# Reordered splits, squares, values and last tile pairs, and shifted convolution bounds, in a two-layer encoder kernel

## The chip, the cores and the metric

One NeuronCore of a Trainium2 chip runs the whole kernel. The metric is the device time of one execution in microseconds (us); the median of several executions is compared.

## What is computed

Two layers of an encoder over 256 positions and 1024 channels, all in fp32. Each layer, cut to what matters here:

```python
h = rmsnorm(x, attn_norm_g[l])
q, k, v, conv_in, gate_logits = jnp.split(h @ w_in[l], SPLITS, axis=-1)
q, k = apply_rope(q), apply_rope(k)            # rotate halves by cos/sin of the positions
y_attn = sliding_window_sink_attention(q, k, v, attn_sinks[l]) @ w_attn_o[l]
ca, cb = jnp.split(conv_in, 2, axis=-1)
u = causal_dwconv(ca * sigmoid(cb), conv_dw_w[l], conv_dw_b[l])      # 31 taps
y_conv = silu(layernorm(u, ...)) @ w_conv_o[l]
x = x + (sigmoid(g_attn) * y_attn + sigmoid(g_conv) * y_conv) @ w_out[l]
up = causal_dwconv(rmsnorm(x) @ w_ffn_up[l], ...)                     # 3 taps
x = x + (silu(gt) * val) @ w_ffn_down[l]
```

A final RMSNorm ends it.

## The kernel before

Weights come in units of 128 x 2048 numbers (16 blocks of 128 x 128), 66 units a layer, through a ring of three slots (`raw`, `whi`, `wlo`; unit u lies in slot u % 3). To keep fp32 accuracy each weight and each activation is split into a high part of type fp32r and the rest: the high part of a weight is `whi` (ScalarE, ACT in the profile, `split_high`, L311), the rest `wlo` (GpSimd, POOL, `split_low`, L250; in the last part of a layer VectorE, DVE, takes two of three, L891). A product of one block is three matmuls (L1034 to L1036): whi with high, whi with low, wlo with high. A unit is 48 matmuls of 256 columns. SyncE loads the next unit into a slot when `wlo` of the one before is written.

Every engine has its own queue of instructions, written out by hand and worked off in order; semaphores tie them. So the order of the lines is the schedule.

Units 0 to 7 give the convolution's input, 8 gives k and v, 9 to 12 give q, 13 to 20 the gates, 21 to 32 the three output projections, 33 to 65 the channel mixer ("FFN"). The steps that the change touches:

- **Start of layer 0.** DVE copies x and writes its low parts, then makes the angles of the rotation (L712 to L716; seven steps counted by the semaphore `table`; unit 2 on TensorE, PE, waits for them at L1191 since they use its bank `pu[2]`), then adds up the squares of x (`add_first_squares`, L692). PE multiplies units 0, 1 and 2 by parts (`unit_by_parts`, L1089) with x as it is; after unit 1 it sums the squares over partitions (`first_total`, L1184). ACT turns the sum into `rstd` (L356), and DVE then scales and normalises x for unit 3 (`normalise`, L655).
- **Rotations.** For k and for four pairs of q tiles, ACT writes the halves exchanged into `pt` (`swap_halves`, L445, four copies) and, behind that, splits the next unit for the slot just read (`next_high`, L317; for some units it also makes two products of a convolution that GpSimd adds up, L343, `tap_product`). DVE rotates (`rotate`, L767: two products and a sum). Between the rotations DVE works on the 31-tap convolution (`conv`, L723; a step is two taps, L749), in numbers of steps set by `CONV_BOUNDS`, one row a layer. In layer 0 ACT also makes sine and cosine after the first exchange.
- **Attention groups 0 to 7.** For each group PE multiplies a gate unit, transposes the probabilities (L1157), and multiplies them with the values of the group before (`values`, L1160). PE makes the scores of two groups at a time (L1146) inside every second gate unit, and waits there for the exponentials of the group before (L1137). DVE takes the maxima and the denominators with `conv` steps between them (7 steps a group in the first groups, 6 in the others, so that all 109 are done; L824).
- **End of a layer.** The last unit (65, slot 2) multiplies the last two hidden tiles (`ab` 0 and 1) into four banks (L1318 to L1327); it waits until both tiles are split. ACT loads the table for the roots, splits slots 0 and 1 for the next layer (L598), then squares x and writes its high parts as each bank is ready; DVE adds x and writes the low parts (L1002 to L1015). GpSimd makes `wlo` of slots 0, 1, 2 in that order.

Of the kernel before, what the change touches and what calls it, by code (L numbers as in the profile page):

```python
# [5 lines left out]
DEPTH, D_MODEL, SEQ = 2, 1024, 256  # L6
# [6 lines left out]
FT = D_FF // P  # L13
N_CHUNKS = SEQ // CHUNK
N_PAIRS = N_HEADS // 2
GROUPS = N_CHUNKS * N_KV
# [7 lines left out]
U_AO, U_CO, U_OUT, U_FFN = 21, 25, 29, 33  # L24
FFN_STEPS = FT // 2
UNITS = U_FFN + 3 * FFN_STEPS
AHEAD = 2
PIECES = 4
PIECE = UNIT // PIECES
UNSCALED = RING  # L30
# [3 lines left out]
USES = UNITS // RING  # L34
# [12 lines left out]
CONV_PAIRS, POOL_TILE, LAST_TILE = ((0, 1), (3, 4), (5, 6)), 2, 7  # L47
FIRST_TAPS = (TAPS + 1) // 2
CONV_STEPS = TAPS * len(CONV_PAIRS) + FIRST_TAPS
CONV_BOUNDS = ((37, 43, 49, 53, 56), (39, 45, 51, 55, 59))  # L50
CONV_DONE = (2 * TAPS, 4 * TAPS, 6 * TAPS, 2 * CONV_STEPS)
PRODUCT_BUFFERS = 3
PRODUCT_UNITS = (7, 8, 9, 10, 11, 12, 14, 16, 17, 18, 19, 20, 21, 22)
# [21 lines left out]
def hybrid_encoder(nc, x_in, pos_in, const_in, par_in, gf_in, w_in, y_out):  # L75
# [3 lines left out]
    with ctx:  # L79
# [98 lines left out]
        def finished(l, u):  # L178

            return uses(l, u) + 1  # L180
# [126 lines left out]
        def _(act):  # L307
# [3 lines left out]
            def split_high(l, s, n):  # L311

                act.wait_ge(raw_in[s], (l * USES + n) * 16)
                act.wait_ge(unit_done[s], l * USES + n)
                A(whi[s][:, :], raw[s][:, :], ACT.Copy).then_inc(hi_ready[s], 1)  # L315

            def next_high(l, u):  # L317
                if u + RING < UNITS:
                    split_high(l, (u + RING) % RING, (u + RING) // RING)
                if u + RING in PRODUCT_UNITS:  # L320
                    n = PRODUCT_UNITS.index(u + RING)
                    if n == 0:
                        tap_product(l, 0)
                    tap_product(l, n + 1)
                    if n == PRODUCTS - 3:
                        tap_product(l, n + 2)
# [84 lines left out]
            for l in range(DEPTH):  # L411
                par = par_all[:, l * NPAR:(l + 1) * NPAR]
                for i in range(NT):
                    u = U_GLU + i
# [30 lines left out]
                def swap_halves(n, src, tiles, scale):  # L445

                    if n:
                        act.wait_ge(rope_done, l * 10 + 2 * n)
                    for block in range(4):
                        rows, other = slice(32 * block, 32 * block + 32), slice(32 * (block ^ 1), 32 * (block ^ 1) + 32)  # L450
                        last = A(pt[rows, 0:tiles, :], src[other], ACT.Copy, scale=scale if block % 2 else -scale)
                    last.then_inc(rot_done, 1)

                u = U_KV
                act.wait_ge(unit_done[u % RING], finished(l, u))
                act.wait_ge(u_ready, l * NT + NT)
                swap_halves(0, pu[u % RING][:, 0:1, :], 1, HEAD_DIM ** -0.5)
                A(kvraw[:, 1, :], pu[u % RING][:, 1, :], ACT.Copy).then_inc(kv_raw, 1)
                next_high(l, u)
                if l == 0:  # L460
                    act.wait_ge(table, TABLE_STEPS)
                    A(sin[:, :], angles, ACT.Sin).then_inc(act_table, 1)
# [3 lines left out]
                for i in range(4):  # L466
                    u = U_Q + i
                    act.wait_ge(unit_done[u % RING], finished(l, u))
                    swap_halves(1 + i, pu[u % RING][:, :, :], 2, 1.0)
                    if i == 1:  # L470
                        act.wait_ge(vt_done, l + 1)
                        A(vwin[0:CHUNK, 0, :], po[0:CHUNK, 0, 0:P], ACT.Copy).then_inc(v_ready, 1)
                        A(vwin[:, 1:N_CHUNKS, :], po[:, :, :].rearrange("p a (b t) -> p (a b) t", t=P)[:, 1:N_CHUNKS, :], ACT.Copy).then_inc(v_ready, 1)
                    next_high(l, u)

                def evict_transposed(n):
                    act.wait_ge(tr_done, l * GROUPS + n + 1)
# [79 lines left out]
                def hidden_tile(k, ab, gcol, vcol, before=None, split=None):  # L557

                    act.wait_ge(up_ready, k + 1)
                    if before is not None:  # L560
                        act.wait_ge(f_ready, before)
                    for half, col in ((0, gcol), (1, vcol)):
                        A(fbuf[:, ab, half, :], up[:, ab, half, :], ACT.Identity, scale=par[:, col + 2:col + 2 + 1],  # L563
                          bias=par[:, col + 3:col + 3 + 1]).then_inc(f_conv0, 1)
                    if split is not None:
                        split()
                    act.wait_ge(f_tap, k * 4 + 3)
                    A(fbuf[:, ab, 2, :], fbuf[:, ab, 0, :], ACT.Silu).then_inc(f_silu, 1)
# [11 lines left out]
                def ffn_step(j, parity, last):  # L580

                    k = j * 2 + l * FT
                    col = j * 8 + PA_FW
                    hidden_tile(k, 0, col, col + FT * 4, k - 1, lambda: split_high(l, 2, j + 11))
                    act.wait_ge(unit_done[1], l * USES + j + 11)
                    hidden_high(k, 0, parity)
                    hidden_tile(k + 1, 1, col + 4, col + FT * 4 + 4, k, None if last else lambda: split_high(l, 0, j + 12))
                    hidden_high(k + 1, 1, parity)
                    if not last:
                        split_high(l, 1, j + 12)  # L590
# [5 lines left out]
                ffn_step(FFN_STEPS - 1, 0, True)  # L596
                load_roots()
                if l < DEPTH - 1:  # L598
                    for s in range(AHEAD):
                        split_high(l, s, USES)  # L600
                for i in range(4):
                    act.wait_ge(x_ready, l * 8 + 4 + i + 1)
                    into = po[:, :, :] if i == 0 and l < DEPTH - 1 else sq[:, 2 * i:2 * i + 2, :]
# [21 lines left out]
        def _(dve):  # L625
# [20 lines left out]
            def gained_low(l, p):  # L646

                dve.wait_ge(uh_ready, l * 12 + p + 1)
                for t in (2 * p, 2 * p + 1):
                    gain = const[:, C_GAIN + l * NT + t:C_GAIN + l * NT + t + 1]  # L650
                    last = V.scalar_tensor_tensor(ul[:, t, :], down[p][:, t % 2, :], gain, uh[:, t, :].bitcast(f32),
                                                  ALU.mult, ALU.subtract)
                last.then_inc(ul_ready, 1)
# [53 lines left out]
            for p in range(NT // 2):  # L707
                dve.wait_ge(x_in_s[min(p, 2)], 16)
                V.tensor_copy(down[p][:, :, :], x[:, 2 * p:2 * p + 2, :]).then_inc(copied, 1)
                dve.wait_ge(copied, p + 1)  # L710
                gained_low(0, p)
            dve.wait_ge(pos_s, 16)  # L712
            step(V.tensor_copy(pu[2][:, 0, :], pos_i))
            step(V.tensor_scalar(ang, pu[2][:, 0, :], const[:, C_FREQ:C_FREQ + 1], None, ALU.mult))
            angle_turns(ANGLE_SCALES[0], pu[2][:, 0, :])
            angle_rest(ANGLE_SCALES[0], pu[2][:, 0, :])  # L716
            add_first_squares(0)
            dve.wait_ge(pad_zero, 1)

            for l in range(DEPTH):  # L720
# [306 lines left out]
        def _(pe):  # L1027
# [61 lines left out]
            def unit_by_parts(s, hi, lo, hi_part, lo_part, then=None):  # L1089

                for p in range(NT // 2):
                    places = [(k, m) for k in (2 * p, 2 * p + 1) for m in range(2)]
                    pe.wait_ge(hi_part, p + 1)
                    pe.wait_ge(hi_ready[s], p + 1)
                    for k, m in places:
                        w = slice((2 * k + m) * P, (2 * k + m + 1) * P)
                        MM(pu[s][:, m, :], whi[s][:, w], hi[:, k, :], start=(k == 0 and m == 0), stop=False, skip_group_check=True)
                    pe.wait_ge(lo_part, p + 1)
                    for k, m in places:
                        w = slice((2 * k + m) * P, (2 * k + m + 1) * P)  # L1100
                        MM(pu[s][:, m, :], whi[s][:, w], lo[:, k, :], start=False, stop=False, skip_group_check=True)
                    pe.wait_ge(lo_ready[s], p + 1)
                    for k, m in places:
                        w = slice((2 * k + m) * P, (2 * k + m + 1) * P)
                        last = MM(pu[s][:, m, :], wlo[s][:, w], hi[:, k, :], start=False, stop=(k == NT - 1), skip_group_check=True)
                last.then_inc(unit_done[s], 1)
                if then is not None:
                    then()

            for _ in range(WARMUPS):  # L1110
                MM(pu[1][:, 0, 0:P], ones[:, :], ones[:, :], start=True, stop=True)
# [3 lines left out]
            for l in range(DEPTH):  # L1115
# [132 lines left out]
                for i in range(GROUPS):  # L1248
                    if i + 1 < GROUPS:
                        standard(U_GATE + i + 1, hh, hl, None, {(1, 0): lambda: scores(i + 1)} if i % 2 else {})  # L1250
                    else:
                        group_half(0, 0)
                    transpose_probs(i)
                    if i:
                        values(i - 1)
                group_half(1, 0)
                values(GROUPS - 1)
# [57 lines left out]
                pe.wait_ge(hi_ready[2], hi_count((l + 1) * USES - 1))  # L1315
                pe.wait_ge(lo_ready[2], lo_count(2, (l + 1) * USES - 1))

                pe.wait_ge(fh_ready, (l + 1) * FT)  # L1318
                pe.wait_ge(fl_ready, (l + 1) * FT)
                for i in range(4):  # L1320
                    for m in (2 * i, 2 * i + 1):
                        for ab in range(2):
                            last = product(down[i][:, m % 2, :], 2, NT * ab + m, fh[:, ab, :], fl[:, ab, :], False, True, True)
                    if i < 3:
                        last.then_inc(down_done, 1)
                    else:
                        last.then_inc(unit_done[2], 1)  # L1327
# [77 lines left out]
```

## Time and profile before

| what | value |
|---|---|
| median of 3 runs | 826.69 us (826.07 to 826.8) |
| the profiled execution's own time | 827.24 us |
| its span, first to last instruction | 825.4 us |
| PE busy with matmuls | 808.1 us (98%), 6820 of them |
| DVE, ACT, POOL busy | 588.8, 518.8, 456.7 us |
| mean granted TensorE clock | 0.997 of full |

Times in the rows are microseconds from the span's start. A row of the timeline is start, duration, engine, line, operation, tiles, shape and count; in brackets stands how long the engine had been idle before it and what ended that. PE's matmuls are pipelined: one of 256 columns starts every 0.12 us though each lasts 0.28.

### The profile page before, as it was taken

To read this page: it belongs to the slowest core of one execution; us is meant where nothing else is said; L and a number is where in the kernel's file an instruction comes from. 1 tells how busy PE (TensorE), PEld (TensorE's weight loads), DVE (VectorE), ACT (ScalarE), POOL (GpSimd) and SP (SyncE) were. 2 spreads that over 40 slices of the span, in tenths; PEclk is the share of its full clock that TensorE was granted. 3 is DMA by queue.
4 is the path that set the end of the run, shared out by engine and by line. 5 is a ranking of instruction groups with operands and counts; after the bars stand their busy time and mean duration, and the time that the engine had idled before them with its cause. 6 is when DMAs were issued, how large, how long until landed. Compare 5 with 4: busy or idle time off the path is not lost.

```text
span 825.4 us, 16620 instructions
## 1 busy us (share of the span) xinstructions
PE 808.1 (98%) x6820; PEld 790.5 (96%) x6820; DVE 588.8 (71%) x1162; ACT 518.8 (63%) x852; POOL 456.7 (55%) x140
## 2 busy tenths in 40 slices
PE   8999999999999999999999999999999999999996
PEld 7999989899999999999999999989999999999995
DVE  5799998583559766666579999876535887665664
ACT  6856798773665655555576587887446654554543
POOL 6898787687722233222289987887875032223220
PEclk9999999999999999999999999999999999999998
DMA  8654444445455655555455544444454456545521
GB/s 288 212 204 148 161 151 150 154 155 189 169 172 185 205 187 177 199 170 188 154 197 168 198 154 154 154 145 151 165 194 165 157 202 204 202 155 201 179 81 52
DMA packets 21386, 142.26 MB, mean 172 GB/s; under 512 B 2624, under 2 KB 3136, under 8 KB 4672
## 3 DMA queue, kind: packets, MB, share of 16 engines
q1 hardware_dynamic: 20592, 140.43, 49.5%
q8 instruction: 54, 0.88, 0.4%
q10 hardware_dynamic: 720, 0.78, 0.3%
q14 instruction: 20, 0.16, 0.1%
HBM read 140.15 MB, written 1.05 MB: 171 GB/s over the span
## 4 chain that ended last, share of the span: by engine, by line
PE 78%; ACT 9%; DVE 8%; issue 2%; DMA 1%; POOL 1%; SPq 0%; DVEq 0%; ACTq 0%
PE pu L1034 21%; PE pu L1035 20%; PE pu L1036 20%; ACT whi L315 4%; DVE wlo L894 3%; PE ps L1034 2%; PE ps L1036 2%; PE ps L1035 2%; DVE pc L749 2%; ACT qk L563 1%; PE pt L1036 1%; PE pt L1035 1%; PE pt L1034 1%; DMA x<-in_x_t 1%; DVE gate L941 1%
## 5 line engine op out<-in xcount | busy, mean ns | idle before, releaser
L253 POOL TENSOR_TENSOR wlo<-raw,whi 128x2048 fp32r<-128x2048 f32 x86 | 397.3, 4624 | 334.0 <-ACT whi L315 333.8
L1034 PE MATMUL pu<-uh,whi 128*128 128x256 f32 x880 | 249.8, 284 | 1.8 <-POOL wlo L253 1.4
L315 ACT ACTIVATE whi<-raw 128x2048 fp32r<-128x2048 f32 x129 | 245.7, 1906 | 8.3 <-PE pu L1036 7.3
L1035 PE MATMUL pu<-ul,whi 128*128 128x256 f32 x880 | 249.0, 283 | 0.0
L1036 PE MATMUL pu<-uh,wlo 128*128 128x256 f32 x880 | 249.0, 283 | 0.0
L1034 PE MATMUL pu<-hh,whi 128*128 128x256 f32 x704 | 201.6, 286 | 2.2 <-POOL wlo L253 1.4
L1035 PE MATMUL pu<-hl,whi 128*128 128x256 f32 x704 | 199.1, 283 | 0.0
L1036 PE MATMUL pu<-hh,wlo 128*128 128x256 f32 x704 | 199.1, 283 | 0.0
L1034 PEld LDWEIGHTS pu<-uh,whi 128*128 128x128 f32 x880 | 168.9, 192 | 2.4 <-issue 2.3
L1035 PEld LDWEIGHTS pu<-ul,whi 128*128 128x128 f32 x880 | 168.9, 192 | 0.1
L1036 PEld LDWEIGHTS pu<-uh,wlo 128*128 128x128 f32 x880 | 168.9, 192 | 0.0
L749 DVE SCALAR_TENSOR_TENSOR pc<-upad,par_all,pc 128x256 f32<-128x256 f32 x404 | 162.9, 481 | 0.1
L1034 PEld LDWEIGHTS pu<-hh,whi 128*128 128x128 f32 x704 | 134.9, 192 | 8.2 <-issue 7.1
L1035 PEld LDWEIGHTS pu<-hl,whi 128*128 128x128 f32 x704 | 135.0, 192 | 0.0
L1036 PEld LDWEIGHTS pu<-hh,wlo 128*128 128x128 f32 x704 | 135.0, 192 | 0.0
L563 ACT ACTIVATE qk<-gate,par_all 128x256 f32<-128x256 f32 x88 | 48.2, 594 | 124.7 <-DVE gate L941 124.7
L894 DVE TENSOR_TENSOR wlo<-raw,whi 128x2048 fp32r<-128x2048 f32 x42 | 95.9, 2284 | 0.0
L955 DVE SCALAR_TENSOR_TENSOR qk<-gate,par_all,qk 128x254 f32<-128x254 f32 (+1 forms) x176 | 73.3, 478 | 30.0 <-ACT qk L563 30.0
L941 DVE TENSOR_TENSOR gate<-pu,rstd 128x512 f32<-128x512 f32 x44 | 30.2, 687 | 63.9 <-PE pu L1036 57.4
L1034 PE MATMUL ps<-oh,whi 128*128 128x256 f32 x176 | 50.0, 284 | 0.5 <-DVE ol L963 0.5
L1036 PE MATMUL ps<-oh,wlo 128*128 128x256 f32 x176 | 49.8, 283 | 0.0
L1035 PE MATMUL ps<-ol,whi 128*128 128x256 f32 x176 | 49.8, 283 | 0.0
(210 smaller groups left out, 1232.9 us busy)
## 6 DMA issues: line engine op xcount, KB each, us to landing
raw<-in_weights SPq DMA_DIRECT2D x130, 1024.0 KB, 4.9
raw<-in_weights SPq DMA_DIRECT2D x3, 512.0 KB, 8.8
x<-in_x_t SPq DMA_DIRECT2D x2, 256.0 KB, 4.8
raw<-in_weights SPq DMA_DIRECT2D x2, 256.0 KB, 3.9
x<-in_x_t SPq DMA_DIRECT2D x1, 512.0 KB, 8.0
out_y<-qk SPq DMA_DIRECT2D x2, 256.0 KB, 2.8
out_y<-qk ACTq DMA_DIRECT2D x2, 256.0 KB, 2.7
par_all<-in_params SPq DMA_DIRECT2D x1, 236.0 KB, 6.9
```

Of the source, the lines that this page charges most:

```text
L253: nc.gpsimd.tensor_tensor(wlo[s][:, :], raw[s][:, :], whi[s][:, :].bitcast(f32), ALU.subtract).then_inc(lo_ready[s], 1)
L315: A(whi[s][:, :], raw[s][:, :], ACT.Copy).then_inc(hi_ready[s], 1)
L563: A(fbuf[:, ab, half, :], up[:, ab, half, :], ACT.Identity, scale=par[:, col + 2:col + 2 + 1], bias=par[:, col + 3:col + 3 + 1]).then_inc( ...
L749: V.scalar_tensor_tensor(out, upad[:, t, k:k + T], w, sums, ALU.mult, ALU.add).then_inc(conv_step, 1)
L894: V.tensor_tensor(wlo[s][:, :], raw[s][:, :], whi[s][:, :].bitcast(f32), ALU.subtract).then_inc(lo_ready[s], 1)
L941: V.tensor_tensor(up[:, ab, :, :], pu[s][:, :, :], rstd[:, :].unsqueeze(1).to_broadcast([P, 2, T]), ALU.mult).then_inc(up_ready, 1)
L955: last = V.scalar_tensor_tensor(acc, up[:, ab, half, 0:T - shift], par[:, col:col + 1], acc, ALU.mult, ALU.add).then_inc(f_tap, 1)
L1034: MM(out, whi[s][:, w], hi, start=start, stop=False, skip_group_check=accumulate)
L1035: MM(out, whi[s][:, w], lo, start=False, stop=False, skip_group_check=accumulate)
L1036: return MM(out, wlo[s][:, w], hi, start=False, stop=stop, skip_group_check=accumulate)
```

## The change

Seven edits of order. (1) In the five rotation steps ACT makes the next unit's split, and the products that hang on it, ahead of exchanging the halves. (2) In layer 0, the split of slot 0 for layer 1 moves into the last hidden tile of the FFN, between its first convolution tap and its SiLU; behind the table load only slot 1's is left. (3) At the start DVE adds the squares ahead of the angles. (4) PE sums the squares inside unit 1, ahead of its last quarter, not behind the unit. (5) Layer 0's convolution bounds fall from 37, 43, 49, 53, 56 to 37, 42, 47, 51, 54, so that two steps fewer lie between the rotations, and two more in the attention groups. (6) In the last attention group the values of group 6 come ahead of the transposes of group 7. (7) The last unit of a layer takes the first hidden tile for both output tiles of the first bank, then the second hidden tile, and waits for the two hidden tiles one at a time.

```diff
-CONV_BOUNDS = ((37, 43, 49, 53, 56), (39, 45, 51, 55, 59))
+CONV_BOUNDS = ((37, 42, 47, 51, 54), (39, 45, 51, 55, 59))
@@ ACT, unit 8
                 act.wait_ge(u_ready, l * NT + NT)
+                next_high(l, u)
                 swap_halves(0, pu[u % RING][:, 0:1, :], 1, HEAD_DIM ** -0.5)
                 A(kvraw[:, 1, :], pu[u % RING][:, 1, :], ACT.Copy).then_inc(kv_raw, 1)
-                next_high(l, u)
@@ ACT, units 9 to 12
                     act.wait_ge(unit_done[u % RING], finished(l, u))
+                    next_high(l, u)
                     swap_halves(1 + i, pu[u % RING][:, :, :], 2, 1.0)
...
-                    next_high(l, u)
@@ ACT, last FFN step
-                    hidden_tile(k + 1, 1, col + 4, col + FT * 4 + 4, k, None if last else lambda: split_high(l, 0, j + 12))
+                    hidden_tile(k + 1, 1, col + 4, col + FT * 4 + 4, k, None if last and l == DEPTH - 1 else lambda: split_high(l, 0, j + 12))
...
                 if l < DEPTH - 1:
-                    for s in range(AHEAD):
-                        split_high(l, s, USES)
+                    split_high(l, 1, USES)
@@ DVE, start
+            add_first_squares(0)
             dve.wait_ge(pos_s, 16)
             step(V.tensor_copy(pu[2][:, 0, :], pos_i))
...
             angle_rest(ANGLE_SCALES[0], pu[2][:, 0, :])
-            add_first_squares(0)
@@ PE, unit_by_parts
+                    if p == 2 and then is not None:
+                        then()
                 last.then_inc(unit_done[s], 1)
-                if then is not None:
-                    then()
@@ PE, groups
+                    if i == GROUPS - 1:
+                        values(i - 1)
                     transpose_probs(i)
-                    if i:
+                    if 0 < i < GROUPS - 1:
                         values(i - 1)
@@ PE, last unit
-                pe.wait_ge(fh_ready, (l + 1) * FT)
-                pe.wait_ge(fl_ready, (l + 1) * FT)
                 for i in range(4):
-                    for m in (2 * i, 2 * i + 1):
-                        for ab in range(2):
+                    for m, ab in ((0, 0), (1, 0), (0, 1), (1, 1)) if i == 0 else ((2 * i, 0), (2 * i, 1), (2 * i + 1, 0), (2 * i + 1, 1)):
+                            if (i, m) == (0, 0):
+                                pe.wait_ge(fh_ready, (l + 1) * FT - 1 + ab)
+                                pe.wait_ge(fl_ready, (l + 1) * FT - 1 + ab)
```

## Rows read from the trace of the kernel before

**Rows 1.** Waits of PE: what for, us in total, times, longest us
```profile
PE pu L1034 <- POOL wlo L253: 2.9, 3, 1.4
PE ps L1146 <- ACT probs L493: 1.6, 1, 1.6
PE pt L1157 <- ACT probs L502: 1.1, 3, 0.4
```

**Rows 2.** Timeline of PE, first 30 us: sum of squares, unit 2's end, unit 3
```profile
21.30 0.60 PE L1186 MATMUL po<-qk,ones 128*128 128x256 f32 x2
...
27.00 0.64 PE L1105 MATMUL pu<-uh,wlo 128*128 128x256 f32 x4
28.23 0.39 PE L1034 MATMUL pu<-hh,whi 128*128 128x256 f32 x1 [0.59 <-DVE upad L689]
```

**Rows 3.** Timeline of ACT, first 30 us: the last square of x
```profile
15.27 0.62 ACT L383 ACTIVATE qk<-x 128x512 f32<-128x512 f32 x1
```

**Rows 4.** Timeline of DVE, first 30 us: angles begin, squares, first scaled product
```profile
14.36 0.42 DVE L713 CAST pu<-probs 128x256 f32<-128x256 int32 x1
...
17.64 1.50 DVE L698 TENSOR_TENSOR po<-qk,po 128x512 f32<-128x512 f32 x2
...
27.77 0.41 DVE L689 SCALAR_TENSOR_TENSOR upad<-kvraw,pu 128x256 f32<-128x256 f32 x1
```

**Rows 5.** Timeline of ACT, layer 0: exchange of q's first pair, split of unit 12
```profile
72.95 2.29 ACT L451 ACTIVATE pt<-pu 32x512 f32<-32x512 f32 x4 [2.64 <-DVE kr L779]
75.17 1.90 ACT L315 ACTIVATE whi<-raw 128x2048 fp32r<-128x2048 f32 x1
```

**Rows 6.** Timeline of DVE, layer 0: rotation of k, then six convolution steps
```profile
70.34 0.43 DVE L775 SCALAR_TENSOR_TENSOR gate<-pu,cos 128x256 f32<-128x256 f32 x1 [0.79 <-ACT cos L465]
...
72.89 4.80 DVE L749 SCALAR_TENSOR_TENSOR pc<-upad,par_all,pc 128x256 f32<-128x256 f32 x12
```

**Rows 7.** Timeline of PE, layer 0: scores of groups 2 and 3
```profile
106.86 1.10 PE L1146 MATMUL ps<-kr,qk 64*64 64x128 f32 x32 [1.62 <-ACT probs L493]
```

**Rows 8.** Windows, 104 to 110 us: busy us (count) of each engine, PEclk, DMA, GB/s
```profile
104.00:110.00 6.00, 4.38 (x60) 4.04 (x59) 5.96 (x17) 5.27 (x18) 5.82 (x2) 1.00 0.37 122
```

**Rows 9.** Timeline of ACT, layer 1: exchange for k, split, products; exponentials of group 1
```profile
468.48 1.44 ACT L451 ACTIVATE pt<-pu 32x256 f32<-32x256 f32 x4 [2.78 <-PE pu L1036]
...
470.23 1.91 ACT L315 ACTIVATE whi<-raw 128x2048 fp32r<-128x2048 f32 x1
472.04 0.89 ACT L343 ACTIVATE qk<-upad,par_all 128x256 f32<-128x256 f32 x2
...
507.23 0.36 ACT L493 ACTIVATE probs<-ps,less_top 128x128 f32<-128x128 f32 x1
```

**Rows 10.** Timeline of DVE, layer 1: rotation of k
```profile
470.64 0.41 DVE L775 SCALAR_TENSOR_TENSOR gate<-pu,cos 128x256 f32<-128x256 f32 x1
```

**Rows 11.** Timeline of PE, layer 1: scores of groups 2 and 3
```profile
507.89 1.10 PE L1146 MATMUL ps<-kr,qk 64*64 64x128 f32 x32
```

**Rows 12.** Timeline of PE, layer 0: transposes of group 7
```profile
152.82 0.66 PE L1157 MATMUL pt<-const,probs 128*128 128x128 f32 x4 [0.45 <-ACT probs L502]
```

**Rows 13.** Timeline of DVE, layer 0: low part of group 5's output
```profile
151.37 0.41 DVE L818 TENSOR_TENSOR ol<-po,oh 128x256 fp32r<-128x256 f32 x1
```

**Rows 14.** Timeline of PE: layer 0's last unit begins, layer 1's first unit begins
```profile
408.57 0.36 PE L1034 MATMUL ps<-oh,whi 128*128 128x256 f32 x1 [0.27 <-DVE ol L963]
...
415.97 0.36 PE L1034 MATMUL pu<-uh,whi 128*128 128x256 f32 x1 [1.41 <-POOL wlo L253]
```

**Rows 15.** Timeline of ACT, end of layer 0: last SiLU, splits of slots 0 and 1
```profile
406.56 0.42 ACT L568 ACTIVATE qk<-qk 128x256 f32<-128x256 f32 x1 [1.34 <-DVE qk L955]
...
409.28 3.72 ACT L315 ACTIVATE whi<-raw 128x2048 fp32r<-128x2048 f32 x2
```

**Rows 16.** Timeline of POOL, end of layer 0: wlo of slots 0 and 1
```profile
411.27 9.18 POOL L253 TENSOR_TENSOR wlo<-raw,whi 128x2048 fp32r<-128x2048 f32 x2 [13.53 <-ACT whi L315]
```

**Rows 17.** Timeline of DVE, end of layer 0: low part of x's first pair
```profile
414.27 0.88 DVE L651 SCALAR_TENSOR_TENSOR ul<-ps,const,uh 128x256 fp32r<-128x256 f32 x2 [1.85 <-ACT uh L372]
```

More of the change, by code:

```diff
@@ L26 @@
 UNITS = U_FFN + 3 * FFN_STEPS
-AHEAD = 2
 PIECES = 4
```

## The prediction

> **What bounds the kernel now.** I read the page first: PE is busy 98% of the span at full clock, so only its stops can be won back. The list of PE's waits names them. The largest are three stops for POOL's `wlo` (2.9 us), one of 1.6 us for the exponentials, and three for scaled probabilities (1.1 us) [rows 1]. Then I went to PE's timeline for each stop, and from there to the queue of the engine it waited for, back to the instruction that set the time. A stop costs slightly more than its idle time, because matmuls start every 0.12 us and a restart is slow: unit 2's last four start at 27.00 and take 0.48, and unit 3 starts at 28.23, which is 0.75 lost where 0.59 is shown as idle [rows 2]. The change touches seven places. I take them in order of time.
>
> **Start (edits 3 and 4).** The additions of the squares run from 17.64 (two, then three shorter ones, 2.8 us in all, an estimate from the two at 1.50), behind the angles that run from 14.36 to 17.64 [rows 4]. The last square is there at 15.27 + 0.62 = 15.9 [rows 3]. In front of the angles the additions end near 17.2. PE takes the sum at 21.30, behind unit 1 [rows 2]. A quarter of a unit is 12 matmuls, 1.43 us, so ahead of the last quarter the sum comes at 19.87, and nothing makes it wait. The angles, 3.28 us, then end at 17.2 + 3.3 = 20.5. Unit 2 waits for them, but starts at 21.6, so this wait is covered by 1.1 us. What hangs on the sum comes 1.43 us earlier: the first scaled product, at 27.77 + 0.41 [rows 4], comes at 26.75. Unit 3 then starts at 27.48, when unit 2 is through. That is 0.75 saved, and since POOL's `wlo` of unit 4 is also nearly late there, up to 1.1. I take 0.9. Lower end 0, if ACT's or POOL's queue holds unit 3 anyway.
>
> **Rotations in layer 0 (edits 1 and 5).** Three things can be late. POOL's `wlo` of unit 12 is late because ACT splits it at 75.17, behind the exchange of 2.29 us, which itself waits for DVE's rotation [rows 5]. With the split first it begins some 4.9 us sooner, right after the cosine, and these stops for POOL go. That alone wins nothing at the end of the stretch, for PE stops again at 106.86 for the exponentials of group 1 [rows 7]. This stop is set by DVE. It works without idle time from the rotation of k, which waits for ACT's cosine [rows 6], through all rotations to the maxima and denominators of group 0, and ACT is full from there to those exponentials. So the stretch gets shorter only by what DVE's chain loses. The cosine stays where it is relative to unit 8: the same split and exchange lie ahead of it, in another order. Two steps are four instructions of 4.80 / 12 = 0.40 us [rows 6], 1.6 us. They come back in groups 5 and 6, where DVE waits for ACT before the denominators, and only 0.3 of them would be felt there, off PE's path. I take 1.6 saved on top of the 0.9. Bounds: 0, if an exchange now comes too late for DVE (it has 0.1 to 2 us of cover in each of the four q rotations, by my walk), and 3.9, all of the stops in this stretch.
>
> **Rotations in layer 1 (edit 1 alone).** Here no cosine hides the new order, and the bounds stay. Today ACT exchanges k's halves at 468.48, copies v, and splits at 470.23 with products behind it to 472.93 [rows 9]. DVE rotates k at 470.64 without having been idle [rows 10]. With the split and the products first (1.81 + 0.89 = 2.70 us) the copy of v ends at 473.03 where it ended at 470.33, and DVE waits until 473.08: 2.44 us idle. Queued behind that wait are all convolution steps and rotations, and DVE has no idle time up to the denominators of group 0. The four exchanges of q stay ahead of DVE, as it is later too. The exponentials of group 1 end at 507.59 [rows 9], and PE comes for them at 507.89 [rows 11], so 0.30 of slack is there at most; about half of it is a signal's own delay (an estimate: the score matmuls' stop in [rows 7] has the same kind). This stretch gets 2.44 - 0.15 = 2.3 us longer, as stops at the transposes of group 0 (some 0.6) and at the scores (the rest). Bounds: 0 and 2.7.
>
> **Values ahead of transposes (edit 6), each layer.** PE idles 0.45 at the transposes of group 7 [rows 12]. The values of group 6 take 0.58. They need the output of group 5 read, by DVE at 151.37 + 0.41 = 151.8 [rows 13], and PE is free at 152.2. They fill the stop: 0.55 each, 1.1 in both layers (bounds 0 and 1.2). Next late is the low part of group 6's output, in front of the values of group 7, with about 0.1 us of cover.
>
> **Last unit (edit 7), each layer.** PE starts it at 408.57 where it could at 408.14, after an idle 0.27 for the low part of the last tile [rows 14]. Six matmuls of the first tile, 0.72 us, now cover that: 0.4 each, 0.8 in both. In layer 0 edit 2 puts a split of 1.8 us ahead of the last SiLU, where ACT had idled 1.34 [rows 15]. The tile comes up to 0.46 later, and the 0.72 just covers it. Bounds 0 and 0.9.
>
> **Boundary of the layers (edit 2).** Layer 1's first unit starts at 415.97, 1.41 us idle for POOL's `wlo` of slot 0 [rows 14], which POOL makes from 411.27 in 9.18 / 2 = 4.6 us [rows 16] behind ACT's split at 409.28 [rows 15]. The split now starts about 405.2, right behind the last tile's first tap, and ends by 407.0; POOL is through by 411.7. The old last unit ends at 408.57 + 48 x 0.12 = 414.35, the new one near 414.0. ACT has one split instead of two ahead of the squares and high parts, so those come 1.86 earlier less 0.4 for the later tile. The low part of the first pair, at 414.27 + 0.88 [rows 17], comes at 413.7, ahead of PE. The later pairs are 0.2 us early each, so this is the new thin spot. I take 1.55 saved. Bounds 0.8 (low parts late) and 1.6.
>
> **Sum.** -0.9 - 1.6 + 2.3 - 1.1 - 0.8 - 1.55 = -3.65 us. The profiled execution goes from 827.24 to 823.6 (span 825.4 to 821.75). It lies 0.55 above the median, so for the median 826.69 - 3.65 = 823.0.
>
> **Rivals.**
> Layer 1 loses nothing: DVE's wait is absorbed on its way to the exponentials. For it speaks that several engines wait on each other there, and one unseen wait less would do. Against it, DVE shows no idle time between k's rotation and the denominators. 823.0 - 2.3 = 820.7.
> Some savings stay away: the low parts hold layer 1's first units, or POOL and ACT hold unit 3. Each costs 0.7 to 0.9: 824.0 or so.
> Layer 0 gains nothing from its shorter chain, because an exchange behind its split meets DVE too late: -3.65 + 1.6 and perhaps a little more, 824.6 to 825.5. This is also the case in which the edits cancel, with layer 1 losing what layer 0 wins.
> Slower: the splits in front of the exchanges make DVE wait at most rotations, in both layers. Place: ACT's queue, units 9 to 12. Price: 2.7 (1.8 without products) less DVE's cover of 0.7 to 2.4, which is 1.5 + 0.3 + 2.0 + 1.1 = 4.9 a layer, 9.8 in all, giving 832.8. It decides from where the splits start about 3 us later than in my walk, as they would if the weights landed late; they now land some 5 us ahead. From 3.65 us of such waits the change is no gain.
> TensorE's clock falls to its lower level (1.2 of 2.4 GHz) behind layer 1's new stop. The stretch with the longest stop before attention, 1.62 us [rows 7], shows a granted clock of 1.00 through it [rows 8], and the new one is of that size. At the lower level each us of matmuls costs one more, so 3.65 us of them eat the gain; with 6 of them it is 825.4. The Trainium skill (TensorE: Matmul & The Clock Gate, Why this matters for your kernels) warns that idle gaps between bursts of matmuls return the clock to its lower level. By that rule a new stop can cost more than its own length; the trace disagrees for stops of this size.
>
> **Chances.** Forecast 0.52 (its own range 822.2 to 823.8). Layer 1 free 0.13. Some savings missing 0.18. Layer 0 gains nothing 0.10. Clock 0.02. Slower 0.05. A measurement of this kernel tells about 0.2% (1.65 us) from no change, so faster means under 825.0. Faster 0.85 (the first three, and a part of the fourth), same 0.09, slower 0.06. Range 820.4 to 825.2: it takes in the first two rivals and most of the third.
>
> **What would show it.** PE's waits without `wlo` of POOL; unit 3 starting near 27.5; in layer 0 the scores of groups 2 and 3 near 104.4, still with a stop of over 1 us; in layer 1 DVE idle 2.4 us ahead of k's rotation, and a stop of about 1.6 us at the scores that was not there; no stop before the values of group 6; layer 1's first unit right behind the last of layer 0. I would be wrong if DVE had idle time between k's rotation and group 0, or if PE's stops moved to low parts at the boundary.

## The result, and the profile after

| | before | after |
|---|---|---|
| median | 826.59 us (826.07 to 827.46, 13 runs) | 828.38 us (827.53 to 829.07, 13 runs) |
| ratio | 1 | 1.0021 (95%: 1.0013 to 1.0029) |
| profiled execution, span | 827.24, 825.4 us | 829.07, 827.3 us |
| mean granted TensorE clock | 0.997 | 0.994 |

The change makes the kernel 1.8 us slower, where 3.65 us less was forecast. The profiled execution is the slowest of the 13 (the fastest, 827.53 us, had a mean clock of 0.997), so its trace shows the loss at its largest. The waits of PE after, in the form of [rows 1] (what for, us in total, times, longest):

```profile
PE ps L1032 <- DVE ol L961: 4.0, 1, 4.0
PE ps L1144 <- ACT probs L492: 3.2, 2, 1.6
PE pt L1155 <- ACT probs L501: 1.4, 2, 0.8
...
PE pu L1032 <- DVE wlo L892: 0.4, 2, 0.2
```

The three stops for POOL's `wlo` are gone, as forecast. A stop of 4 us stands in their place, for the low part of a hidden tile. PE's timeline shows where: in the last unit of layer 0, behind the six matmuls of the first tile (compare [rows 14]; line numbers are two lower after the change).

```profile
403.98 0.28 PE L1032 MATMUL ps<-oh,whi 128*128 128x256 f32 x1
...
404.58 0.28 PE L1034 MATMUL ps<-oh,wlo 128*128 128x256 f32 x1
408.82 0.55 PE L1032 MATMUL ps<-oh,whi 128*128 128x256 f32 x1 [3.97 <-DVE ol L961]
...
409.60 0.41 PE L1032 MATMUL ps<-oh,whi 128*128 128x256 f32 x1
...
410.24 0.41 PE L1032 MATMUL ps<-oh,whi 128*128 128x256 f32 x1
```

Behind the stop three matmuls take 0.64 us, 0.21 each, where they take 0.12 elsewhere. The windows say why. Columns are busy us (count) of PE, its weight loads, DVE, ACT and POOL, then the granted clock, the DMA share and GB/s:

```profile
404.90:408.60 3.70, 0.00 (x0) 0.00 (x0) 3.22 (x2) 0.78 (x2) 2.58 (x1) 0.89 0.15 20
409.00:414.00 5.00, 5.00 (x24) 5.00 (x25) 1.66 (x3) 3.89 (x6) 2.48 (x1) 0.50 0.44 184
415.00:420.00 5.00, 5.00 (x44) 5.00 (x43) 4.21 (x9) 4.03 (x8) 1.10 (x1) 1.00 0.59 198
```

After standing still for 4 us, TensorE gets half its clock (1.2 of 2.4 GHz): 24 matmuls in 5 us, not 44. Some 27 matmuls of the last unit start 0.21 us apart and not 0.12, 27 x 0.09 = 2.4 us more.

DVE's timeline, then POOL's, show what the low part waited for:

```profile
403.28 4.49 DVE L957 SCALAR_TENSOR_TENSOR qk<-qk 128x256 f32<-128x256 f32 x1 [0.52 <-ACT qk L567]
408.25 0.43 DVE L961 SCALAR_TENSOR_TENSOR ol<-qk,oh 128x256 fp32r<-128x256 f32 x1 [0.48 <-ACT oh L571]
```
```profile
402.94 4.54 POOL L252 TENSOR_TENSOR wlo<-raw,whi 128x2048 fp32r<-128x2048 f32 x1 [9.37 <-ACT whi L314]
```

DVE's product of the last hidden tile (L957) lasts 4.49 us, not 0.42. It begins 0.34 us after POOL's subtraction begins and ends 0.29 us after that ends. In the kernel before, that subtraction began at 411.27 [rows 16], when this product was long over. Edit 2 put it 8.3 us earlier, on top of the product.

**Where the time went**, as differences of the two profiles at the same instructions. PE's timeline after, in order: sum of squares, unit 3, scores of groups 2 and 3, layer 1's first unit:

```profile
18.85 0.60 PE L1184 MATMUL po<-qk,ones 128*128 128x256 f32 x2
...
26.47 0.28 PE L1032 MATMUL pu<-hh,whi 128*128 128x256 f32 x1
...
103.33 1.10 PE L1144 MATMUL ps<-kr,qk 64*64 64x128 f32 x32 [1.61 <-ACT probs L492]
...
416.47 0.28 PE L1032 MATMUL pu<-uh,whi 128*128 128x256 f32 x1
```

The first matmul of unit 3 comes 1.76 us earlier (26.47, [rows 2]). The scores of groups 2 and 3 come 3.53 us earlier (103.33, [rows 7]), and the last unit of layer 0 starts 4.59 earlier (403.98, [rows 14]). Up to here the change wins. Layer 1's first unit starts 0.5 us later (416.47, [rows 14]), so the boundary alone turned 4.6 us won into a loss. At layer 1's scores it is 2.97 us later (510.86, [rows 11]), and at the end 1.9, after layer 1's own gains (0.65 from the scores to its FFN, 0.42 from there to its last unit).

### The profile page after: what moved, and what is told of

Read it like the earlier page. It is cut to its first block, busy times and chain, and to the rows that moved or that the text cites. A ratio compares the mean times of both kernels' runs of the same rounds, so it can differ in the third digit from the quotient of the medians.

```text
span 827.3 us, 16614 instructions
## 1 busy us (share of the span) xinstructions
PE 809.0 (98%) x6820; PEld 792.6 (96%) x6820; DVE 592.8 (72%) x1162; ACT 519.4 (63%) x852; POOL 456.4 (55%) x140
## 4 chain that ended last, share of the span: by engine, by line
PE 78%; DVE 11%; ACT 7%; issue 2%; DMA 1%; SPq 0%; DVEq 0%; ACTq 0%
PE pu L1032 20%; PE pu L1033 20%; PE pu L1034 20%; DVE pc L747 4%; ACT whi L314 3%; DVE wlo L892 2%; PE ps L1032 2%; PE ps L1033 2%; PE ps L1034 2%; PE po L1166 1%; PE pt L1033 1%; PE pt L1032 1%; PE pt L1034 1%; PE pc L1033 1%; PE pc L1034 1%
```

## The experiments

Theory 1: POOL's subtraction, which reads SBUF, keeps DVE's product of two SBUF tiles waiting for its whole length, and TensorE's clock falls in the stop. Theory 2: the moved split delays the last tile through ACT's queue or in some other way, and POOL has no part in it. Each kernel ran beside the kernel before on the same chip; a ratio is to it. Its median beside them was 826.3 to 826.4 us.

**Edit 2 undone** (e1):

```diff
-None if last and l == DEPTH - 1 else lambda: split_high(l, 0, j + 12)
+None if last else lambda: split_high(l, 0, j + 12)
-                    split_high(l, 1, USES)
+                    for s in range(2):
+                        split_high(l, s, USES)
```

> The changed kernel with the split of slot 0 back behind the table load (edit 2 undone), all else as changed. Theory 1 (GpSimd's subtraction, started early by edit 2, holds back DVE's product of two SBUF tiles for its whole length, and TensorE's clock falls in the stop that this makes): the 4 us stop in the last unit goes, the clock stays up, 828.4 - 5.0 = 823.4 us. Theory 2 (the split itself delays the last tile through ACT): the same 823.4. So this run only shows that edit 2 holds the loss; if it stays above 826, the loss lies elsewhere.

Measured 825.87 us (824.08 to 827.52, 10 runs), ratio 0.9992 (0.9983 to 1.0001). The 4 us stop is gone, and the one for `wlo` is back, longer than in [rows 14]:

```profile
413.52 0.36 PE L1033 MATMUL pu<-uh,whi 128*128 128x256 f32 x1 [1.89 <-POOL wlo L252]
```

The stop is longer since PE now ends the last unit 0.4 sooner, but ACT and POOL are no sooner: without edit 2, edit 7 wins nothing in layer 0. From the stop early in layer 0's FFN to layer 1's scores this kernel takes 507.99 - 255.88 = 252.1 us, the changed one 510.86 - 254.15 = 256.7. That is 4.6 less, of the 5.0 expected. The median is 2.5 us better and not 5, because the first 30 us came out worse in the profiled execution, which lies near the median: unit 3 starts at 28.20 here and at 26.47 in the changed kernel, with the same instructions up to there. A third of a microsecond of this is there when PE takes up the third piece of x (11.31 against 10.98). The other 1.4 is TensorE's clock, in the same window of this kernel, then of the changed one:

```profile
13.40:16.70 3.30, 3.30 (x17) 3.30 (x17) 3.06 (x7) 3.19 (x7) 3.30 (x4) 0.50 0.97 390
```
```profile
13.40:16.70 3.30, 3.30 (x30) 3.28 (x29) 3.02 (x8) 2.85 (x6) 3.30 (x4) 1.00 1.00 404
```

The spread over ten runs is 3.4 us, and it goes with the mean clock: 0.998 or 0.999 in the three fastest (824.08 to 824.81 us), 0.994 in the slowest (827.52). That the others lost their time in the same place isn't shown, since one run was profiled. So edit 2 holds the loss, but its size is better read from the traces than from this median.

**POOL waits for the low part** (e2):

```diff
                 if l < DEPTH - 1:
+                    pool.wait_ge(fl_ready, (l + 1) * FT)
                     for s in range(RING):
                         split_low(s, l * USES + USES)
```

> The changed kernel, where GpSimd waits for the low part of the last hidden tile before it starts wlo of slot 0 for layer 1; ACT's split stays early. Theory 1: DVE's product takes 0.42 us and not 4.49, no stop of 4 us, clock at full, GpSimd from about 404.9 to 409.5 and still ahead of layer 1; 828.4 - 6.6 = 821.8 us. Theory 2: nothing moves, 828.4 us or later.

Measured 822.81 us (822.31 to 823.26), ratio 0.9956 (0.9941 to 0.9971). The split stays where edit 2 put it, so theory 2 falls. DVE, then POOL:

```profile
403.09 0.43 DVE L958 SCALAR_TENSOR_TENSOR qk<-qk 128x256 f32<-128x256 f32 x1 [0.52 <-ACT qk L568]
404.00 0.43 DVE L962 SCALAR_TENSOR_TENSOR ol<-qk,oh 128x256 fp32r<-128x256 f32 x1 [0.48 <-ACT oh L572]
```
```profile
404.51 9.22 POOL L252 TENSOR_TENSOR wlo<-raw,whi 128x2048 fp32r<-128x2048 f32 x2 [11.12 <-DVE ol L962]
```

Both DVE instructions are short, POOL starts behind them, and its `wlo` is still ahead of layer 1, whose first unit starts near 409.6 with no stop. From the stop early in layer 0's FFN to layer 1's scores it takes 504.09 - 253.96 = 250.1 us, 6.6 less than the changed kernel, as expected. The medians differ by 5.6 only, because the profiled execution of the changed kernel is the slowest of its 13 and the one of this kernel the fastest of its four. With the collision gone the boundary itself is as forecast: from the start of the last unit to layer 1's first unit it takes 409.69 - 403.79 = 5.90 us, where it took 7.40 [rows 14], so 1.50 saved of the 1.55. This one wait gives the forecast's time, 823.0, to 0.2 us.

**SiLU and product of the last tile in PSUM** (e3):

```diff
-V.scalar_tensor_tensor(fbuf[:, ab, 3, :], fbuf[:, ab, 2, :], 1.0, fbuf[:, ab, 1, :], ...)
+V.scalar_tensor_tensor(hidden_of(k, ab), silu_of(k, ab), 1.0, fbuf[:, ab, 1, :], ...)
+def silu_of(k, ab): return po[:, 0, :] if k == FT - 1 else fbuf[:, ab, 2, :]
+def hidden_of(k, ab): return po[:, 1, :] if k == FT - 1 else fbuf[:, ab, 3, :]
```

ACT writes and reads the same two places, and the low part reads the second. `k` counts on through both layers, so the edit takes hold in layer 0 only, where the collision is; the expectation speaks of each layer.

> The changed kernel, where the SiLU and the product of the last hidden tile of each layer lie in PSUM, so that DVE's product and its low part have one operand in SBUF each; GpSimd's subtraction stays where the change puts it, beside them. Theory 1: DVE's product takes about 0.4 to 0.5 us beside GpSimd's running subtraction, 821.8 us. If it is not the two SBUF operands but any DVE work beside GpSimd, or theory 2: product still 4.5 us, 828.4 us.

Measured 822.62 us (822.2 to 822.96), ratio 0.9955 (0.9938 to 0.9971). POOL, then DVE:

```profile
402.91 9.22 POOL L260 TENSOR_TENSOR wlo<-raw,whi 128x2048 fp32r<-128x2048 f32 x2 [9.37 <-ACT whi L322]
```
```profile
403.21 0.43 DVE L965 SCALAR_TENSOR_TENSOR po<-po,qk 128x256 f32<-128x256 f32 x1 [0.48 <-ACT po L575]
404.09 0.42 DVE L969 SCALAR_TENSOR_TENSOR ol<-po,oh 128x256 fp32r<-128x256 f32 x1 [0.45 <-ACT oh L579]
```

Both run in full beside the subtraction, the product 0.30 us behind its start (0.34 in the changed kernel). From the FFN's early stop to layer 1's scores this kernel takes 250.06 us, e2 250.13. So it is not DVE work beside POOL that blocks. For the product the result moved to PSUM as well as an operand; the low part (L969) still writes SBUF (`ol`), and the next run, where it reads two tiles there instead of one, blocks it. What decides is DVE's second operand in SBUF.

**POOL waits for the product only** (e6):

```diff
+                    pool.wait_ge(f_ready, (l + 1) * FT)
```

> The changed kernel, where GpSimd waits only for DVE's last product, not for the low part behind it. The low part also reads two tiles in SBUF. If two SBUF operands against a GpSimd subtraction under way are what blocks: the product takes 0.43 us and the low part, begun under the subtraction, about 4.5 us; PE's stop stays at about 4 us, 828.5 us. If only this product is touchy, for whatever reason: 822.8 us.

Measured 827.81 us in its one run. DVE, then POOL:

```profile
403.12 0.43 DVE L958 SCALAR_TENSOR_TENSOR qk<-qk 128x256 f32<-128x256 f32 x1 [0.52 <-ACT qk L568]
404.03 4.41 DVE L962 SCALAR_TENSOR_TENSOR ol<-qk,oh 128x256 fp32r<-128x256 f32 x1 [0.48 <-ACT oh L572]
```
```profile
403.63 9.24 POOL L252 TENSOR_TENSOR wlo<-raw,whi 128x2048 fp32r<-128x2048 f32 x2 [10.21 <-DVE qk L958]
```

The block moves to the next instruction with two SBUF operands, and PE stops for 3.89 us. It lets go at 408.4, after the first of POOL's two subtractions (9.24 / 2 = 4.6 us), and not after both. The clock falls here too, but later and for a shorter time:

```profile
409.10:412.40 3.30, 3.30 (x18) 3.30 (x17) 0.70 (x1) 1.33 (x3) 3.30 (x1) 0.50 0.92 318
```

**PE kept busy through the stop** (e4):

```diff
+if (i, m, ab) == (0, 0, 1) and l == 0:
+    for _ in range(30):
+        MM(pu[1][:, 0, :], whi[2][:, 0:P], fh[:, 0, :], start=True, stop=True, skip_group_check=True)
```

> The changed kernel with 30 matmuls of 256 columns, results unused, put into PE's 4 us stop of the last unit in layer 0. If the lower clock behind the stop is a cost of its own: matmuls of the last unit start every 0.12 us and not every 0.21, 828.4 - 2.8 = 825.6 us, with the product still 4.5 us long. If the slow matmuls come from something else (PSUM or operands shared with DVE and ACT): 828.4 us.

Measured 826.53 us (826.07 to 828.53), ratio 1.0004 (0.9995 to 1.0014), 1.85 less than the changed kernel. Windows, the same stretches as above:

```profile
404.90:408.60 3.70, 3.44 (x29) 3.24 (x27) 3.22 (x2) 0.82 (x2) 2.55 (x1) 1.00 0.14 22
409.00:414.00 5.00, 5.00 (x43) 5.00 (x43) 2.72 (x5) 4.85 (x8) 2.51 (x1) 1.00 0.46 185
```

The tile is as late as before (the next real matmul starts at 408.78), yet the clock stays up and 43 matmuls run in the 5 us. From the FFN's early stop to layer 1's scores it is 2.45 us shorter than the changed kernel (508.30 - 254.04 = 254.26 against 256.71). That is the price of the lower clock by itself in these two executions (1.85 at the medians); the stop's own price is the other part.

**Edit 2 alone, on the kernel before** (e5; the diff is its two places in the change's diff):

> The kernel before with edit 2 alone. If GpSimd's early subtraction holds back DVE's product and nothing else is needed for it: product about 4.5 us, the last unit starts 4.9 us later, its matmuls run at the lower clock for about 2.8 us more, and the 1.6 us stop for wlo goes: 826.3 + 6 = 832 us. If the loss needs the other edits as well (the earlier low part of edit 7 for one): near 826.

Measured 831.49 us (830.47 to 831.71), ratio 1.0057 (1.0044 to 1.0071). The product lasts 4.47 us, and PE stops for longer:

```profile
411.81 0.55 PE L1033 MATMUL ps<-oh,whi 128*128 128x256 f32 x1 [4.66 <-DVE ol L962]
```

Edit 2 needs no other edit to do its harm, some 5.1 us.

**K exchanged first in layer 1** (e7, with e2's wait):

```diff
-                next_high(l, u)
+                if l == 0:
+                    next_high(l, u)
                 swap_halves(0, ...)
                 A(kvraw[:, 1, :], pu[u % RING][:, 1, :], ACT.Copy).then_inc(kv_raw, 1)
+                if l:
+                    next_high(l, u)
```

> GpSimd waits for the low part of the last hidden tile (as in the run before of that edit, 822.8 us), and in layer 1 k's halves are exchanged ahead of the split and its products, as in the kernel before; in layer 0, and for q, the split stays first. If DVE's idle time ahead of k's rotation is what costs layer 1 its 2.5 us: it goes, with both stops at group 0 and at the scores, 820.3 us. If the order at q's rotations costs it: 822.8 us, with the stops still there.

Measured 821.46 us (820.97 to 822.79), ratio 0.9941 (0.9928 to 0.9955): 1.35 less than e2, not 2.5, and 1.04 by the traces (399.89 us between the early stops of the two FFNs, 400.93 in e2). DVE no longer waits ahead of k's rotation, but it does ahead of q's first:

```profile
467.03 4.80 DVE L751 SCALAR_TENSOR_TENSOR pc<-upad,par_all,pc 128x256 f32<-128x256 f32 x12
473.31 0.69 DVE L777 SCALAR_TENSOR_TENSOR gate<-pu,cos 128x512 f32<-128x512 f32 x1 [1.48 <-ACT pt L451]
```

DVE's lateness at k had covered the late exchange of q. With the first gone the second shows, as a stop of 1.44 us at the scores. **One convolution step less** (e8, on e7, bounds 37, 42, 47, 50, 53 for layer 0):

> The same as that with one convolution step fewer ahead of layer 0's last two rotations (bounds 37, 42, 47, 50, 53), so that all eight groups have seven steps. If DVE's chain alone sets layer 0's stops at group 0 and at the scores: 0.8 us less than the run before it, 819.5 us. If ACT's exchanges of the last pairs are as late as DVE by now: no difference to it.

Measured 820.73 us (820.68 to 821.06), ratio 0.9931 (0.9918 to 0.9943), 0.7 less than e7, of the 0.8 that two of DVE's 0.4 us instructions make. **Old order in all of layer 1** (e9, on e8; `next_high` behind the exchange for q too when `l` is 1):

> The run with bounds 37, 42, 47, 50, 53 (820.7 us), but with all five rotation steps of layer 1 in the order of the kernel before; only layer 0 keeps the splits first. In that run the trace still shows DVE idle for 1.48 us ahead of q's first rotation in layer 1, and PE stopped for 1.44 us at the scores. If the split and products ahead of that exchange are the cause: both go, 820.7 - 1.4 = 819.3 us. If layer 1's scores are late since PE reaches them earlier after the shorter boundary: the stop stays and the time too, 820.7 us.

Measured 819.62 us (819.24 to 821.24), ratio 0.9925 (0.9911 to 0.9939). That is 1.1 less than e8 (1.49 by the traces, 398.39 us between the early stops of the two FFNs against 399.88). PE's waits, all of them:

```profile
PE ps L1151 <- ACT probs L499: 1.6, 1, 1.6
PE pu L1102 <- ACT uh L372: 1.3, 2, 1.1
PE pu L1116 <- POOL quarter L247: 1.1, 1, 1.1
PE pu L1106 <- DVE ul L656: 0.5, 2, 0.2
PE pu L1039 <- DVE wlo L899: 0.4, 2, 0.2
PE pt L1162 <- ACT probs L508: 0.2, 1, 0.2
```

The stops of 1.6 and 0.2 us for `probs` are layer 0's; layer 1 has none left in attention. This version is 0.75% faster than the kernel before, and faster than the changed one.

## Why the prediction was wrong

**The step that failed** is the boundary (edit 2): "I take 1.55 saved", with bounds 0.8 and 1.6. The run of edit 2 alone gives it a cost of 5.1 us, and in the changed kernel the boundary costs 5.1 (4.59 won before it, 0.5 lost behind it). The parts of the 5.1 are 4.1 for the stop (404.70 to 408.82), 2.45 for the clock, and 1.5 saved. I followed ACT's split, POOL's start and PE's need correctly: POOL starts at 402.94, 8.3 earlier than before, and e2 shows the saving. What was false is "The tile comes up to 0.46 later, and the 0.72 just covers it". From the FFN's early stop to the end of the last low part it is 150.12 us in e1, 150.47 in e2, where only ACT's split is in the way, and 154.53 in the changed kernel. The split costs 0.35, and the meeting with POOL, which the prediction put at nothing, 4.06. I did not ask what DVE does while POOL is at work there, and I bounded the step as if moved work could only be late, never stand in another engine's way.

The kernel keeps these two apart nearly everywhere: in the rotations and groups DVE's convolution reads one operand from PSUM, and in the FFN POOL has one unit in three. Where they do meet, the trace of before shows the block, off the path. Of the 44 low parts of hidden tiles (L963) 18 begin under a subtraction of POOL, and each of the 18 ends 0.28 or 0.29 us after that subtraction ends, however much of it was left. Three of them, early in layer 0's FFN, then POOL:

```profile
258.79 4.42 DVE L963 SCALAR_TENSOR_TENSOR ol<-qk,oh 128x256 fp32r<-128x256 f32 x1
...
276.47 2.73 DVE L963 SCALAR_TENSOR_TENSOR ol<-qk,oh 128x256 fp32r<-128x256 f32 x1
...
293.75 1.44 DVE L963 SCALAR_TENSOR_TENSOR ol<-qk,oh 128x256 fp32r<-128x256 f32 x1
```
```profile
258.31 4.62 POOL L253 TENSOR_TENSOR wlo<-raw,whi 128x2048 fp32r<-128x2048 f32 x1 [26.54 <-ACT whi L315]
...
274.29 4.63 POOL L253 TENSOR_TENSOR wlo<-raw,whi 128x2048 fp32r<-128x2048 f32 x1 [11.36 <-ACT whi L315]
...
290.30 4.61 POOL L253 TENSOR_TENSOR wlo<-raw,whi 128x2048 fp32r<-128x2048 f32 x1 [11.37 <-ACT whi L315]
```

A 0.42 us instruction that lasts 4.42, 2.73 or 1.44, on the very line of the last tile's low part. I read that line's usual length and never its longest. The Trainium skill states the rule (SBUF — State Buffer, Who interferes with whom): "A DVE instruction with two SBUF inputs contends with a GpSimd instruction that reads SBUF"; the one that issues first holds the shared pair of ports for its whole instruction. All runs here agree: 4.41 to 4.49 us for the later DVE instruction, and no effect with one operand in PSUM. POOL's subtraction reads and writes SBUF, and no run here tells which of the two it is. By the first of the rows above the tile would have come 4.42 - 0.42 = 4.0 us later, with its cover already spent on the split, so a stop of about 4 us could have been read before the run; 3.97 was measured.

**The clock** was a rival with chance 0.02, weighed at a stop of 1.62 us. It was right that a stop can cost more than its own length, and wrong on the place: the two stops of 1.6 us in attention left the clock at 1.00, and the 4 us one brought it to 0.50 and cost 2.45. The rival's own sum doesn't hold: at one more us for each us of matmuls, 6 of them give 829.0 and not 825.4, and the rate measured is 0.21 against 0.12 a matmul, 0.75 more. The Trainium skill's warning about idle gaps (TensorE: Matmul & The Clock Gate, Why this matters for your kernels) holds at 3.97 us. The prediction said that the trace disagrees with it for stops of 1.62 us; the page warns of longer gaps, so those rows don't speak against it. What no stop of that length explains is e1, where the clock fell at 13.3 us and the longest stop shortly before was 1.30; the kernel before had one of 1.61 us in the same part and kept its clock. What tells the two apart stays open.

**Start: right.** From the place where the sum of squares came or now comes (19.87, 18.85) to unit 3 it was 8.36 and is 7.62 us, 0.74 less of the 0.9 taken. The other 1.0 of the 1.76 is the landing of x, which no edit touches:

```profile
x<-in_x_t SPq DMA_DIRECT2D x1, 512.0 KB, 6.9
```

In the kernel before that load took 8.0 us, and PE stood still for 2.0 us in the first 13 for `uh`, which is made from x; in the changed one 0.9. The run of edit 2 alone has the start of before, landed x in 6.8 us, and began unit 3 at 27.06, 1.17 earlier than before. So this 1 us belongs to the execution and not to the change. **Layer 0's rotations: right.** 3.53 - 1.76 = 1.77 us, 1.6 forecast; a stop for the exponentials of 1.61 us remains, as forecast. **Values ahead of transposes: right.** From the scores to the FFN's early stop 4.16 - 3.53 = 0.63 in layer 0 and 0.65 in layer 1 (0.55 each forecast; the two make 1.28, just above the bound of 1.2). **Last unit: right**, 4.59 - 4.16 = 0.43 in layer 0 and 0.42 in layer 1 (0.4 each), but e1 shows that it counts in layer 0 only with edit 2. **Layer 1's rotations: right.** The loss from the boundary to the scores is 2.97 - 0.50 = 2.5 us, 2.3 forecast, and DVE idles as described against [rows 10]:

```profile
473.69 0.42 DVE L773 SCALAR_TENSOR_TENSOR gate<-pu,cos 128x256 f32<-128x256 f32 x1 [2.52 <-ACT kvraw L458]
```

The stops stand where they were forecast, at the transposes of group 0 (some 0.6) and at the scores:

```profile
505.72 0.66 PE L1155 MATMUL pt<-const,probs 128*128 128x128 f32 x4 [0.63 <-ACT probs L501]
510.86 1.10 PE L1144 MATMUL ps<-kr,qk 64*64 64x128 f32 x32 [1.62 <-ACT probs L492]
```

The forecast kept q's exchanges in layer 1 ahead of DVE, "as it is later too". That condition carries weight: e7 shows that without DVE's lateness the first exchange is 1.5 us late.

So five of the six terms of the sum held, and the sixth held but for the collision. With the boundary as e2 shows it and the other five from the changed kernel's trace, the six make -3.7 us, where -3.65 was forecast. The misses of 0.05 to 0.2 us each cancel, and that part is luck. The range failed because each bound was drawn for the step alone. None was drawn for two engines meeting.

## What to carry to other kernels

When an instruction moves, list what every other engine has under way in its new place, and look in the trace for the longest, not the usual, duration of each of those lines. A few outliers that all end with another engine's instruction give the price of a collision. A GpSimd instruction that reads SBUF belongs beside DVE work that takes one operand from PSUM, or a semaphore has to keep it off. A reorder that is safe where another wait hides it (the cosine in layer 0) can be a plain loss in the loop's next pass: check each layer by itself.

## What the runs showed of the hardware

- A DVE instruction that reads two SBUF tiles, begun under a GpSimd subtraction of 128x2048, lasted until 0.2 to 0.3 us after that subtraction's end: 4.49, 4.47 and 4.41 us for work of 0.42 when begun 0.3 to 0.4 us into it, 2.73 when begun 2.2 us into it, 1.44 at 3.5. With one operand in PSUM it took 0.43 beside the same subtraction. The profile shows it as busy all that time.
- It got through between two GpSimd subtractions issued back to back (4.41 us against 9.24 for both).
- After 3.97 us without a matmul TensorE ran at half clock, 0.21 us a matmul, for nearly 6 us; after 3.89 us (e6) for 3.4. After 1.62 us in attention it did not, but early in e1 it did for 3.4 us with no stop over 1.30. Thirty unused matmuls in the 4 us gap kept the full clock and saved 2.45 us by the traces.
- The first 30 us differ between executions by 1 to 2 us, as much as the effect under study: x landed in 8.0 us before and in 6.8 to 7.3 in the other profiles, and in e1 the low clock added 1.4. Differences between two instructions later in the same trace are free of it.
